# Two hybrid blocks on one core: padded rows, other banks for turned rows, an earlier overflow test, and an end by halves

## The chip, the cores and the metric

The kernel runs on one core of a Trainium2 chip (trn2). The core has five engines with a queue each: TensorE (PE: matrix products), VectorE (DVE), ScalarE (ACT), GpSimd (POOL) and SyncE (SP, which here only issues DMAs), and 16 DMA engines. They meet only through semaphores. The metric is the time of one launch in microseconds on the device, the median of the runs; lower is better.

## The reference

256 tokens of width 1024 in float32 pass through two blocks. Cut to what matters:

```python
def rms_norm(x, g):
    y = x * lax.rsqrt(jnp.mean(x * x, axis=-1, keepdims=True) + EPS)
    return y * g

def first_block(x, ...):
    h = rms_norm(x, g_mix)
    x = x + hybrid_mixer(h, w_in, ...)     # h @ w_in, two kinds of attention, gates, w_pa, w_pb, w_o
    h = rms_norm(x, g_moe)
    x = x + hier_moe(h, ...)               # top 2 of 32 experts for each token
    return rms_norm(x, g_final)

def expert_block(xblk, e):
    return (jax.nn.silu(xblk @ w1[e]) * (xblk @ w3[e])) @ w2[e]

def hybrid_layer(x, c, ...):               # the second block
    shift, scale, gate = jnp.split(silu(c) @ w_ada + b_ada, 3, axis=-1)
    h = rmsnorm(x, norm_g) * (1 + scale) + shift
    proj = h @ w_in                        # 1024 x 10240
    merged = sigmoid(m_attn) * y_attn + sigmoid(m_conv) * y_conv
    return x + gate * (merged @ w_out)

out = rmsnorm(hybrid_layer(first_block(x)), final_g)
```

## The kernel before

One program, 256 tokens as two row blocks (`n` = 0, 1) of 128. Each weight matrix comes by SP into one of five ring buffers of 2 MB (eight in the experts' part), in the order of the list `chunks`. SP issues the next load when the last user of the buffer has raised its semaphore.

*Precision by halves.* A projection's weights are cut into pieces of 128 x 1024. ACT copies a piece to a high part in fp32r (`split_high`, L1881); DVE, or GpSimd for every fourth, subtracts it from the piece to give the low part (`split_low`, L1300 on DVE, L2256 on GpSimd). TensorE multiplies high by high, high by low and low by high (`product`).

*Order.* `Order` objects `O1` (first block) and `O2` (second) are lists of steps written by hand in the Python code. Each engine's program walks the same list and takes its part of each step: TensorE multiplies, ACT and DVE evict and split. A step's place in the list sets its place in each engine's queue. `PB.use(name, bank)` gives a result one of the eight PSUM banks in turn; before TensorE writes a bank it waits until the last result in it has been read (`may_write`: semaphore `free`).

*Start.* SP loads `ident`, the two row blocks of x, `rows` (113 short vectors of 128 numbers packed as rows: gains, biases, convolution weights), then the first projection `fq` in two halves. ACT squares row block 0, DVE row block 1, GpSimd takes the inverse roots (L2244), ACT and DVE scale. TensorE first turns `rows` into columns (`col`), multiplies `ident` by itself before and after (`warm`), then turns x in four pairs (`turn1`). ACT scales each pair with the gain in `col` to the high part (L1890), DVE makes the low part (L1306). DVE copies `col` ahead of scaling row block 1.

*Experts.* Each expert has 64 slots. TensorE gathers tokens, multiplies with w1 and w3, turns, multiplies with w2 (`down`) and scatters pairs of experts into banks 2 to 5. If an expert has more tokens than slots, three more rounds of all experts follow; each engine reads the number (`flag`) and branches around that long code. ACT and DVE did this between the last expert (31) and its finish: `finish` (L2071, L2078) evicts the last down-projection on ACT, `last_low` makes its low part on DVE.

*End.* The last projection `w_out_2` comes in halves `wx0` and `wx1` of 512 columns; both need a bank per row block. DVE multiplies by the gate and adds x, GpSimd (`wx0`) or DVE (`wx1`) multiplies by the last gain, ACT squares (L2162). Then `final` takes the mean squares, GpSimd the roots, ACT scales row block 0 (L2234) and half of 1 (L2236), DVE the other half, SP stores (L890).

## Time and profile before

| | before |
|---|---|
| median of 3 runs | 1033.22 us (1032.62 to 1033.77) |
| profiled execution | 1032.23 us |
| its span | 1030.4 us |
| TensorE busy (PE) | 988.3 us, 96% |
| DVE / ACT / GpSimd busy | 392.5 / 377.1 / 121.8 us |
| mean granted TensorE clock | 0.988 of 2.4 GHz |
| DMA | 308.07 MB, mean 299 GB/s |
| chain that ended last | PE 85%, DVE 7%, ACT 4%, issue 2%, POOL 1%, DMA 1% |

The span runs from the first to the last instruction of the profile; the execution's own time has 1.8 us around it. All lines of product are in helpers: L782 is any matmul, L1300 any product or sum of two tensors on DVE, L1303 and L1306 the forms with a scalar; a row is told by its tiles and its time. "issue" is time for which the profile shows nothing that the engine waits for. `PEld` is the loading of TensorE's stationary operand. A float32 product of `ident` by itself leaves two records.

### The profile page before, as it was taken

To read this page: it belongs to the slowest core of one execution; us is meant where nothing else is said; L and a number is where in the kernel's file an instruction comes from. 1 tells how busy PE (TensorE), PEld (TensorE's weight loads), DVE (VectorE), ACT (ScalarE), POOL (GpSimd) and SP (SyncE) were. 2 spreads that over 40 slices of the span, in tenths; PEclk is the share of its full clock that TensorE was granted. 3 is DMA by queue.
4 is the path that set the end of the run, shared out by engine and by line. 5 is a ranking of instruction groups with operands and counts; after the bars stand their busy time and mean duration, and the time that the engine had idled before them with its cause. 6 is when DMAs were issued, how large, how long until landed. Compare 5 with 4: busy or idle time off the path is not lost.

```text
span 1030.4 us, 16914 instructions
## 1 busy us (share of the span) xinstructions
PE 988.3 (96%) x7393; PEld 767.3 (74%) x7393; DVE 392.5 (38%) x750; ACT 377.1 (37%) x612; POOL 121.8 (12%) x81
## 2 busy tenths in 40 slices
PE   7999999999999999979999999989999999999996
PEld 6888789976555555545555555558989999999995
DVE  4446456853222111121222111127335444774475
ACT  4545646641111111111111111226445555554443
POOL 2110021020000000000000000002321111441122
PEclk8999999999999999998999999999999999999999
DMA  8974295788999999999999999997545544445301
GB/s 271 365 273 177 96 346 217 300 315 348 424 426 425 423 425 426 426 420 426 424 425 423 427 425 424 424 401 283 184 163 187 187 171 164 164 167 204 141 1 42
DMA packets 74829, 308.07 MB, mean 299 GB/s; under 512 B 5585, under 2 KB 12146, under 8 KB 58362
## 3 DMA queue, kind: packets, MB, share of 16 engines
q1 hardware_dynamic: 70962, 302.16, 74.0%
q10 hardware_dynamic: 3784, 4.73, 1.4%
q8 instruction: 61, 1.00, 0.4%
q14 instruction: 22, 0.18, 0.1%
HBM read 305.82 MB, written 2.63 MB: 299 GB/s over the span
## 4 chain that ended last, share of the span: by engine, by line
PE 85%; DVE 7%; ACT 4%; issue 2%; POOL 1%; DMA 1%; SPq 0%; ACTq 0%; DVEq 0%
PE bank L782 82%; DVE arena L1306 3%; DVE arena L1303 2%; PE bank L1251 1%; ACT arena L2058 1%; DVE wR L1300 1%; DMA arena<-in_rows 1%; PE bank L993 1%; DVE arena L1300 1%; ACT wR L1881 1%; POOL wR L2256 1%; ACT arena L2088 0%; DVE hTR L1300 0%; ACT arena L2086 0%; ACT arena L2111 0%
## 5 line engine op out<-in xcount | busy, mean ns | idle before, releaser
L782 PE MATMUL bank<-hTR,wR 128*128 128x256 f32 x2520 | 313.8, 284 | 4.2 <-DVE wR L1300 1.2
L782 PEld LDWEIGHTS bank<-hTR,wR 128*128 128x128 f32 x2520 | 305.1, 192 | 8.2 <-issue 4.2
L782 PE MATMUL bank<-ring,arena 128*64 128x256 f32 (+3 forms) x1680 | 229.6, 439 | 7.1 <-issue 7.1
L1300 DVE TENSOR_TENSOR wR<-ring,wR 128x1024 fp32r<-128x1024 f32 x126 | 157.8, 1259 | 133.2 <-ACT wR L1881 132.6
L1881 ACT ACTIVATE wR<-ring 128x1024 fp32r<-128x1024 f32 x161 | 168.5, 1055 | 109.2 <-PE bank L782 107.4
L782 PEld LDWEIGHTS bank<-ring,arena 128*64 128x64 f32 (+2 forms) x1680 | 115.3, 137 | 103.1 <-issue 59.7
L782 PE MATMUL bank<-arena 128*64 128x256 f32 (+7 forms) x1178 | 166.5, 406 | 0.7 <-DVE small L1432 0.7
L1306 DVE SCALAR_TENSOR_TENSOR arena<-bank,small,arena 128x256 f32<-128x256 f32 x32 | 15.5, 484 | 346.9 <-ACT arena L2058 346.9
L2029 ACT ACTIVATE arena<-bank,small 64x512 f32<-64x512 f32 x62 | 42.4, 684 | 280.5 <-PE bank L782 280.1
L782 PEld LDWEIGHTS bank<-arena 128*64 128x64 f32 (+3 forms) x1178 | 92.3, 144 | 62.4 <-issue 28.3
L2256 POOL TENSOR_TENSOR wR<-ring,wR 128x1024 fp32r<-128x1024 f32 x35 | 85.5, 2443 | 321.7 <-ACT wR L1881 321.7
L2244 POOL TENSOR_TENSOR small<-small,mhalf 128x1 f32<-128x1 f32 (+1 forms) x12 | 8.2, 683 | 479.9 <-DVE small L1306 475.5
L2058 ACT ACTIVATE arena<-bank,small 128x256 f32<-128x256 f32 x32 | 15.2, 475 | 82.7 <-PE bank L782 82.7
L782 PE MATMUL bank<-wR,hTR 128*128 128x512 f32 x192 | 45.2, 393 | 0.0
L782 PEld LDWEIGHTS bank<-wR,hTR 128*128 128x128 f32 x192 | 35.6, 188 | 8.1 <-issue 0.8
L782 PE MATMUL bank<-PmR,XShR 128*128 128x256 f32 x128 | 35.9, 312 | 0.4 <-DVE small L1492 0.3
L782 PEld LDWEIGHTS bank<-PmR,XShR 128*128 128x128 f32 x128 | 24.8, 193 | 11.9 <-issue 11.2
L782 PE MATMUL bank<-PmR,XSlR 128*128 128x256 f32 x128 | 32.7, 287 | 0.0
L1303 DVE TENSOR_SCALAR arena<-bank,col 128x256 f32<-128x256 f32 x64 | 28.1, 477 | 3.4 <-PE bank L782 3.4
L1300 DVE TENSOR_TENSOR arena<-arena 128x512 f32<-128x512 f32 (+5 forms) x36 | 21.4, 604 | 10.8 <-ACT arena L2188 9.8
L1300 DVE TENSOR_TENSOR arena<-bank,arena 128x512 f32<-128x512 f32 (+2 forms) x30 | 19.6, 665 | 15.0 <-PE bank L782 12.7
L782 PEld LDWEIGHTS bank<-PmR,XSlR 128*128 128x128 f32 x128 | 25.0, 195 | 0.0
(209 smaller groups left out, 823.2 us busy)
## 6 DMA issues: line engine op xcount, KB each, us to landing
ring<-in_w SPq DMA_DIRECT2D x39, 2048.0 KB, 21.5
ring<-in_w_in SPq DMA_DIRECT2D x29, 2048.0 KB, 8.4
arena<-in_w SPq DMA_DIRECT2D x25, 2048.0 KB, 19.0
ring<-in_w SPq DMA_DIRECT2D x42, 1024.0 KB, 19.4
arena<-in_w SPq DMA_DIRECT2D x22, 1024.0 KB, 20.9
ring<-in_w_ada SPq DMA_DIRECT2D x6, 2048.0 KB, 7.9
ring<-in_w_o SPq DMA_DIRECT2D x2, 2048.0 KB, 12.4
ring<-in_w_o_attn SPq DMA_DIRECT2D x2, 2048.0 KB, 7.9
```

Of the source, the lines that this page charges most:

```text
L782: return pe.e.matmul(o, l, r, start=start, stop=stop)
L993: last = eng.transpose(banks[u.bank][:, 128 * c:128 * c + 128], P[:, 128 * c:128 * c + 128], ident[:, :])
L1251: last = eng.transpose(banks[x.bank][:, 128 * c:128 * c + 128], Hb[e % 2][:, c:256:2], ident[:, :])
L1300: return eng.tensor_tensor(o, a, b, op)
L1303: return eng.tensor_scalar(o, a, s1, s2, op0) if op1 is None else eng.tensor_scalar(o, a, s1, s2, op0, op1)
L1306: return eng.scalar_tensor_tensor(out=o, in0=a, scalar=s, in1=b, op0=op0, op1=op1)
L1881: eng.activation(h, w, ACT.Copy).then_inc(s_high, 1)
L2029: last = eng.activation(Y[h0:h0 + 64, 512 * h:512 * h + 512], banks[u.bank][64 * h:64 * h + 64, :], ACT.Copy, scale=RW[64 * h:64 * h + 64, ...
L2058: eng.activation(Hb[e % 2], banks[u.bank][:, 0:256], ACT.Silu, scale=RW[:, e // EB % 2, e % EB, 1:2]).then_inc(S["silu"], 1)
L2244: eng.tensor_tensor(o, a, mhalf[:, 0:a.shape[1]], ALU.pow).then_inc(after, 1)
L2256: eng.tensor_tensor(l, pieces[i][1], h.bitcast(F32), ALU.subtract).then_inc(low[i][0], 1)
```

## The change

- `rows` is padded on the host with zeros to 128 rows; SP loads all 128. `ident` is loaded by ACT, ahead of its first instruction, no longer by SP. The second warm-up has 3 products instead of 5.
- The turned pairs of both blocks (`hT1`, `hT3`) take banks 2 to 5, one each; before, they took 0, 1, 6 and 0 in turn. All later results that share banks 0, 1 and 6 shift by one in their turn.
- ACT and DVE test for overflow ahead of expert 31. Its code stands in both branches. TensorE's, SP's and GpSimd's tests stay.
- At the end, `wx0`'s two row blocks come one before and one behind the last weight piece's low part on DVE. For `wx1`, row block 0 is finished to its root before row block 1 is begun; ACT scales row block 0 before it squares the last half of row block 1.

```diff
         for j2 in range(4):
-            PB.use(("hT1", j2), PR.next())
+            PB.use(("hT1", j2), 2 + j2)
...
-            PB.use(("hT3", j2), PR.next())
+            PB.use(("hT3", j2), 2 + j2)
...
-        last4 = list(O2.chunk("wx1", uses, "m"))
+        last4 = O2.chunk("wx1", uses, "m")
+        first = next(last4)
+        O2.add("gate_rows", 0, 0)
+        last4 = [first] + list(last4)
+        O2.add("gate_rows", 0, 1)
         O2.add("evict", "wx0", None)
...
-        O2.add("evict", "wx1", None)
+        for n in range(NT):
+            O2.add("gate_rows", 1, n)
+            O2.add("last_squares", n)
...
         def sync_program(eng):
-            eng.dma_start(ident[:, :], t["k_ident"]).then_inc(s_ident, 16)
...
-            eng.dma_start(VR[0:NROW, :], t["rows"]).then_inc(s_rows, 16)
+            eng.dma_start(VR[:, :], t["rows"]).then_inc(s_rows, 16)
...
-            warm(pe, banks[6], 5)
+            warm(pe, banks[6], 3)
...
+                elif what == "gate_rows":
+                    c, n = a
+                    cs, u = slice(512 * c, 512 * c + 512), U_[f"wx{c}", n]
+                    filled(v, u)
+                    if c:
+                        v.wait_ge(s_gx[n], 1)
+                    tt(GT[n], banks[u.bank][:, :], grow[:, cs], ALU.mult).then_inc(u.free, 1)
+                    emptied(v, u)
+                    v.wait_ge(s_x2done[n], 1)
+                    tt(XN[:, n, cs], GT[n], XN[:, n, cs], ALU.add).then_inc(s_gx[n], 1)
+                    if c:
+                        v.wait_ge(s_gx[n], 2)
+                        v.wait_ge(s_fg, 16)
+                        v.step(tt(XO[:, n, cs], XN[:, n, cs], fg[:, cs], ALU.mult))
+                        final(n)
...
-            last_low = experts(0, PB, dict(zip(MOE_SEMS, [sem(n) for n in MOE_SEMS])))
+            S = {n: sem(n) for n in MOE_SEMS}
+            experts(0, PB, S, 0, NE - 1)
             v.wait_ge(s_flag, 1)
             with eng.If(eng.value_load(flag[0:1, 0:1]) > SLOTS):
-                last_low()
+                experts(0, PB, S, NE - 1)()
...
             with eng.Else():
-                last_low()
+                experts(0, PB, S, NE - 1)()
...
+                elif what == "last_squares":
+                    n = a[0]
+                    squares(1, n)
+                    if n == 0:
+                        s.wait_ge(s_rs[0], 4)
+                        s.wait_ge(s_fo[0], 1)
+                        eng.activation(XO[:, 0, :], XO[:, 0, :], ACT.Copy, scale=st3[:, 6:7]).then_inc(s_out[0], 2)
...
+            eng.dma_start(ident[:, :], t["k_ident"]).then_inc(s_ident, 16)
...
-            finish = experts(0, PB, dict(zip(MOE_SEMS, [sem(n) for n in MOE_SEMS])))
+            experts(0, PB, S, 0, NE - 1)
...
-    arrays["rows"] = np.concatenate([arrays.pop(n).reshape(-1, 128) for n in _ROWS])
+    rows = np.concatenate([arrays.pop(n).reshape(-1, 128) for n in _ROWS])
+    arrays["rows"] = np.concatenate([rows, np.zeros((128 - len(rows), 128), rows.dtype)])
```

The load of `ident` is taken out of SP's program and stands first in ACT's. The changed kernel's own line numbers are a few higher (L782 becomes L788, L1881 L1886).

TensorE's queue at the start, before: `ident,arena` are transposes, `hTR,wR` the first projection; `freeN` is the semaphore of PSUM bank N.

```order
L900 MATMUL bank<-ident,arena 128x113 [waits rows]
L782 MATMUL bank<-ident 128x128 x5
L987 MATMUL bank<-ident,arena 128x128 [waits norm0]
L987 MATMUL bank<-ident,arena 128x128
L987 MATMUL bank<-ident,arena 128x128 [waits norm1]
L987 MATMUL bank<-ident,arena 128x128 x9
L987 MATMUL bank<-ident,arena 128x128 [waits free0]
L987 MATMUL bank<-ident,arena 128x128 x3
L782 MATMUL bank<-hTR,wR 128x256 [waits low_dve,free1]
```

And TensorE's queue at the same place in the changed kernel:

```order
L905 MATMUL bank<-ident,arena 128x113 [waits rows]
L788 MATMUL bank<-ident 128x128 x3
L992 MATMUL bank<-ident,arena 128x128 [waits norm0]
L992 MATMUL bank<-ident,arena 128x128
L992 MATMUL bank<-ident,arena 128x128 [waits norm1]
L992 MATMUL bank<-ident,arena 128x128 x13
L788 MATMUL bank<-hTR,wR 128x256 [waits free2,low_dve]
L788 MATMUL bank<-hTR,wR 128x256 x5
L788 MATMUL bank<-hTR,wR 128x256 [waits free3]
```

No transpose waits for a bank any more, and the first product waits for the first pair (bank 2) instead of the second (bank 1).

ACT's queue round the last expert, before: L2029 evicts a down-projection, L2058 is the silu of an expert, L2038 fills the rows of gains, L2071 evicts the last down-projection.

```order
L2058 ACTIVATE arena<-bank,small 128x256 [waits full0,full6]
L2038 ACTIVATE arena<-bank 128x512 [waits full1]
L2029 ACTIVATE arena<-bank,small 64x512 [waits scat,full7]
L2029 ACTIVATE arena<-bank,small 64x512
L2058 ACTIVATE arena<-bank,small 128x256 [waits full0,full6]
L2038 ACTIVATE arena<-bank 128x512 [waits full0]
L2214 TENSOR_LOAD flag [waits flag]
L2214 COMPARE_AND_BRANCH
L2071 ACTIVATE arena<-bank,small 64x512 [waits full7]
```

And ACT's queue there now:

```order
L2064 ACTIVATE arena<-bank,small 128x256 [waits full0,full6]
L2044 ACTIVATE arena<-bank 128x512 [waits full1]
L2231 TENSOR_LOAD flag [waits flag]
L2231 COMPARE_AND_BRANCH
L2035 ACTIVATE arena<-bank,small 64x512 [waits scat,full7]
L2035 ACTIVATE arena<-bank,small 64x512
L2064 ACTIVATE arena<-bank,small 128x256 [waits full0,full6]
L2044 ACTIVATE arena<-bank 128x512 [waits full0]
L2077 ACTIVATE arena<-bank,small 64x512 [waits full7]
```

The test moved ahead of four instructions, to behind expert 30. On DVE it moved likewise ahead of the last expert's two.

DVE's queue at the end, before: `high` is the last weight piece, `full3` and `full4` are `wx0`, `full0` and `full1` `wx1`, `sq3_n` a row block's squares.

```order
L1300 TENSOR_TENSOR wR<-ring,wR 128x1024 [waits high] x5
L1300 TENSOR_TENSOR arena<-bank,arena 128x512 [waits full3]
L1300 TENSOR_TENSOR arena<-arena 128x512 [waits x2done0,free3]
L1300 TENSOR_TENSOR arena<-bank,arena 128x512 [waits full4]
L1300 TENSOR_TENSOR arena<-arena 128x512 [waits x2done1,free4]
...
L1300 TENSOR_TENSOR arena<-bank,arena 128x512 [waits gx1,full1]
L1300 TENSOR_TENSOR arena<-arena 128x512 [waits free1]
L1300 TENSOR_TENSOR arena<-arena 128x512 [waits gx1]
L1300 TENSOR_TENSOR small<-small 128x1 [waits sq3_0]
```

And DVE's queue at the end now; `wx0` is in banks 2 and 3, `wx1` in 4 and 0:

```order
L1305 TENSOR_TENSOR wR<-ring,wR 128x1024 [waits high] x4
L1305 TENSOR_TENSOR arena<-bank,arena 128x512 [waits full2]
L1305 TENSOR_TENSOR arena<-arena 128x512 [waits x2done0,free2]
L1305 TENSOR_TENSOR wR<-ring,wR 128x1024 [waits high]
L1305 TENSOR_TENSOR arena<-bank,arena 128x512 [waits full3]
...
L1305 TENSOR_TENSOR small<-small 128x1 [waits sq3_0]
L1308 TENSOR_SCALAR small<-small 128x1 [waits dve_own]
L1305 TENSOR_TENSOR arena<-bank,arena 128x512 [waits gx1,full0]
L1305 TENSOR_TENSOR arena<-arena 128x512 [waits free0]
```

The last low part now stands behind the first half of `wx0`, and row block 1 of `wx1` behind row block 0's small steps.

## Rows read from the trace of the kernel before

**Rows 1.** Stretch: us; busy PE, PEld, DVE, ACT, POOL; granted clock; DMA share, GB/s.

```profile
600.00:650.00 50.00, 48.96 (x390) 29.51 (x390) 10.63 (x28) 8.90 (x15) 0.00 (x0) 1.00 1.01 425
```

**Rows 2.** Chain of waits, 0 to 40 us: start us, us, what.

```profile
0.72 0.39 SPq L846
...
2.11 7.54 DMA arena<-in_rows
...
10.14 2.16 PE bank L782 x10
12.30 0.87 PE bank L987 x4
...
13.26 0.85 ACT hTR L1890 x2
...
16.30 0.80 DVE hTR L1306 x2
...
17.14 22.93 PE bank L782 x189
```

**Rows 3.** DMA issues of the page: size of one, us from issue to landing.

```profile
out_x<-arena SPq DMA_DIRECT2D x2, 512.0 KB, 3.0
...
ident<-in_k_ident SPq DMA_DIRECT2D x1, 64.0 KB, 2.0
```

**Rows 4.** Timeline of the start: start us, us, engine, line, operation [idle before].

```profile
4.92 1.06 ACT L2205 ACTIVATE arena<-arena 128x1024 f32<-128x1024 f32 x1 [2.92 <-DMA arena<-in_x]
...
6.40 1.23 DVE L1817 CUSTOM_DVE_ANT_0 arena<-arena 128x1024 f32<-128x1024 f32 x1 [6.40 <-DMA arena<-in_x]
...
8.41 0.56 POOL L2244 TENSOR_TENSOR small<-small,mhalf 128x1 f32<-128x1 f32 x1
...
10.37 0.74 DVE L1303 TENSOR_SCALAR arena<-arena,small 128x1024 f32<-128x1024 f32 x1
```

**Rows 5.** Loads from w_in issued in 2.4 to 3.0 us.

```profile
DMA to landing us min/median/max: 10.1/10.1/10.1
```

**Rows 6.** Busy time as in rows 1, at the start.

```profile
12.00:14.00 2.00, 2.00 (x11) 2.00 (x11) 0.00 (x0) 0.74 (x3) 0.00 (x0) 0.50 1.04 387
```

**Rows 7.** Timeline round the last expert.

```profile
680.79 1.38 ACT L2029 ACTIVATE arena<-bank,small 64x512 f32<-64x512 f32 x2 [7.65 <-PE bank L782]
...
686.94 0.48 DVE L1306 SCALAR_TENSOR_TENSOR arena<-bank,small,arena 128x256 f32<-128x256 f32 x1 [10.78 <-ACT arena L2058]
...
688.54 3.65 PE L782 MATMUL bank<-ring,arena 128*64 128x512 f32 x16 [0.56 <-issue]
...
693.47 0.68 ACT L2071 ACTIVATE arena<-bank,small 64x512 f32<-64x512 f32 x1 [5.36 <-issue]
```

**Rows 8.** Who waited for whom, 450 to 680 us: us in total, times, longest.

```profile
PE bank L782 <- issue: 6.5, 1, 6.5
```

**Rows 9.** Timeline of the end.

```profile
1014.60 1.23 DVE L1300 TENSOR_TENSOR wR<-ring,wR 128x1024 fp32r<-128x1024 f32 x1 [1.49 <-ACT wR L1881]
...
1017.78 1.28 DVE L1300 TENSOR_TENSOR arena<-arena 128x512 f32<-128x512 f32 x1
...
1019.15 1.29 POOL L2313 TENSOR_TENSOR arena<-arena 128x512 f32<-128x512 f32 x1 [0.63 <-DVE arena L1300]
...
1021.66 0.69 DVE L1300 TENSOR_TENSOR arena<-bank,arena 128x512 f32<-128x512 f32 x1
1022.39 1.42 DVE L1300 TENSOR_TENSOR arena<-arena 128x512 f32<-128x512 f32 x2
...
1024.14 1.09 POOL L2244 TENSOR_TENSOR small<-small,mhalf 128x1 f32<-128x1 f32 x2 [3.70 <-DVE small L1303]
...
1024.80 1.15 ACT L2234 ACTIVATE arena<-arena,small 128x1024 f32<-128x1024 f32 x1 [0.96 <-issue]
...
1025.85 0.71 ACT L2236 ACTIVATE arena<-arena,small 128x512 f32<-128x512 f32 x1
```

**Rows 10.** From the page: matmuls of 512 columns, busy us, mean ns.

```profile
L782 PE MATMUL bank<-wR,hTR 128*128 128x512 f32 x192 | 45.2, 393 | 0.0
```

More of the change, by code:

```diff
@@ L1577, in weights, with experts @@
                 tt(WR[:, :, :, 0], S01[0], S01[1], ALU.add).then_inc(s_weights, 1)
-            def experts(r, P, S):
+            def experts(r, P, S, lo=0, hi=NE):
                 g = max(r - 1, 0)
@@ L1609, in experts @@
                     select(0)
-                for j in range(4):
-                    gathered(0, j)
-                if not r:
-                    weights()
-                for e in range(NE):
+                if lo == 0:
+                    for j in range(4):
+                        gathered(0, j)
+                    if not r:
+                        weights()
+                for e in range(lo, hi):
                     b, k = divmod(e, EB)
@@ L1725, in second_steps @@
                            ALU.mult).then_inc(u.free, 1)
-                    elif nm in ("wx0", "wx1"):
-                        c = int(nm[2])
-                        cs = slice(512 * c, 512 * c + 512)
-                        for n in range(NT):
-                            u = U_[nm, n]
-                            filled(v, u)
-                            if c:
-                                v.wait_ge(s_gx[n], 1)
-                            tt(GT[n], banks[u.bank][:, :], grow[:, cs], ALU.mult).then_inc(u.free, 1)
-                            emptied(v, u)
-                            v.wait_ge(s_x2done[n], 1)
-                            tt(XN[:, n, cs], GT[n], XN[:, n, cs], ALU.add).then_inc(s_gx[n], 1)
-                            if c:
-                                v.wait_ge(s_gx[n], 2)
-                                v.wait_ge(s_fg, 16)
-                                v.step(tt(XO[:, n, cs], XN[:, n, cs], fg[:, cs], ALU.mult))
+                elif what == "gate_rows":
[13 more added lines that the diff above has]
+                        final(n)
                 elif what == "norm2":
@@ L1851, in vector_program @@
                     second_steps(*step)
-            final()
         def scalar_program(eng):
@@ L2018, in route, with experts @@
                 eng.activation(ex5, ex5, ACT.Exp).then_inc(s_rexp, 1)
-            def experts(r, P, S):
+            def experts(r, P, S, lo=0, hi=NE):
                 g = max(r - 1, 0)
@@ L2046, in high @@
                         eng.activation(YhR[par][:, cs], Yb[par][:, cs], ACT.Copy).then_inc(S["yhigh"], 1)
-                for e in range(NE):
+                for e in range(lo, hi):
                     if e:
@@ L2090, in second_norm, with squares @@
                 eng.activation(XV[:, 0, :], XS2[:, 0, :], ACT.Copy, scale=tw[:, 10:11]).then_inc(s_norm[0], 1)
+            def squares(c, n):
+                s.wait_ge(s_gx[n], c + 1)
+                if c:
+                    s.wait_ge(s_sq3[n], 1)
+                eng.activation(JK[n], XN[:, n, 512 * c:512 * c + 512], ACT.Square,
+                               accum_out=st3[:, 2 * n + c:2 * n + c + 1]).then_inc(s_sq3[n], 1)
             def bias(h):
@@ L2210, in scalar_program @@
             route()
-            finish = experts(0, PB, dict(zip(MOE_SEMS, [sem(n) for n in MOE_SEMS])))
+            S = {n: sem(n) for n in MOE_SEMS}
+            experts(0, PB, S, 0, NE - 1)
             s.wait_ge(s_flag, 1)
@@ L2214, in scalar_program @@
             with eng.If(eng.value_load(flag[0:1, 0:1]) > SLOTS):
-                finish()
+                experts(0, PB, S, NE - 1)()
                 s.wait_ge(s_scat, NE // 2)
@@ L2223, in scalar_program @@
             with eng.Else():
-                finish()
+                experts(0, PB, S, NE - 1)()
             s.known = known
@@ L2231, in scalar_program @@
                     second_steps(*step)
-            s.wait_ge(s_rs[0], 4)
-            s.wait_ge(s_fo[0], 1)
-            eng.activation(XO[:, 0, :], XO[:, 0, :], ACT.Copy, scale=st3[:, 6:7]).then_inc(s_out[0], 2)
             s.wait_ge(s_rs[1], 4)
```

30 lines of the change are left out of this document (12 added, 18 removed).

## The prediction

> **What bounds the kernel now.** I read the stretches of engine time first, then the chain of waits at the start, the timeline round the last expert, and the timeline of the end. In the experts' stretch TensorE is busy for 48.96 of 50 us, and the DMA engines are full too, share 1.01 at 425 GB/s [rows 1]. TensorE has no spare time there, and the change adds and removes nothing there; so from about 17 us to the end of the last expert the kernel is one long train behind TensorE, and what moves its first wagon moves all of it. What the change can win lies in three places where TensorE waits or is done: before its first projection, between the last expert's product and the last scatter, and after its last matmul.
>
> *The start.* TensorE starts its projections at 17.14 us [rows 2]. The chain back from there [rows 2] is: the load of `rows` (7.54 us, landed at 9.65), its transpose, warm-up products until 12.30, transposes of x, ACT's scaling at 13.26, DVE's low part of the first weight piece (to 16.30), DVE's second pair of `hTR`. Nothing in it is long because of arithmetic; the load is. It is 113 rows of 512 bytes, fewer than the 128 of `ident` (64 KB), which lands 2.0 us after its issue [rows 3].
>
> *The last expert.* ACT waits 5.36 us before the last down-projection is evicted, and the reason shown is "issue": nothing that the profile sees. TensorE has had that product ready since 688.54 + 3.65 = 692.19; ACT starts at 693.47 [rows 7].
>
> *The end.* TensorE's last product has ended when DVE begins at 1021.66. Then DVE (three products, to 1023.81), ACT's square, DVE's two small steps, GpSimd's two square roots (1.09 us, to 1025.23), ACT's scaling of row block 0 (1.15) and only then half of row block 1 (0.71, to 1026.56), and the last store [rows 9].
>
> **Part 1: start.** Edits that answer together: `rows` on 128 partitions, `ident` issued by ACT, three warm-up products instead of five, own banks.
> - `rows` stands behind both loads of x. x0 comes to use at 4.92 us, x1 at 6.40 [rows 4]. If `rows` spreads as `ident` does, it lands right behind x1, at about 6.5 less what x gains; as now, it lands at 9.65. I take the first: 113 rows of 512 bytes took 7.54 us, 128 rows of the same length 2.0.
> - The Trainium skill (DMA: Bandwidth & Descriptors, "Why a DMA increments its semaphore by 16 and not by 1") says that the number of DMA engines is the largest up to 16 that divides the outer sizes: one for 113 partitions, sixteen for 128. The row cannot tell one slow engine from queueing behind x; by the rule the whole excess over x goes, and so does the same engine's lateness in what follows.
> - That lateness matters: the first half of `fq`, issued at 2.49, takes 10.1 us to land (12.6 us) [rows 5]. Were it still that late, less the 0.4 that SP gains below, ACT could split it at 12.2; now it does so behind its first two scalings, at 13.26 + 0.85 = 14.1 [rows 2], so the chain would win only 1.9 us. Spread, the bytes before it are 64 + 1024 + 64 + 1024 KB, and at the 387 GB/s of rows 6 these 2.2 MB take 5.8 us. Issued from 1.1 us on, with the 2.0 of a small load ahead, it lands near 9.
> - `ident` away from SP: x is issued 0.39 + 0.06 us earlier [rows 2]. `ident` still shares the engines (64 of 576 KB), so x gains 0.25 to 0.45; I take 0.4. ACT has a spare 2 us before x arrives, so its own issue (0.4 us) is hidden; without that cover it would cost 0.4.
> - New critical path: x, squares, GpSimd's roots. The second root ends at 8.41 + 0.56 = 8.97 now, 8.57 then. DVE scales at once instead of at 10.37 (it stands behind the copy of `rows`): 8.62 + 0.74 = 9.36 [rows 4]. TensorE transposes the first four blocks by 9.85 (four take 0.87 us [rows 2], and only two of the four wait for DVE). ACT's first scaling starts at 9.9 instead of 13.26, 3.4 us earlier. DVE and ACT then do what they did: the low part of piece 0 ends at 12.9 instead of 16.30.
> - Warm-up: nine products of 0.43 us (2.16 for ten halves, rows 2) from 2.8 to 6.7, the transpose of `rows`, three more to about 8.4; TensorE then idles under 1 us before x is ready. Two fewer products win nothing themselves (they end before x is ready); they must only not delay.
> - Own banks: now the first product waits for bank 1, so for DVE's pair at 17.10, though its weights are ready at 16.30. Then it waits for the weights and pair 0 alone and starts at 12.9. But pairs 1 to 3 arrive every 0.80 us [rows 2], while six matmuls last 0.73 (22.93 / 189 each), so the first tile ends with DVE's last pair, 15.35 + 0.75 = 16.1, instead of 17.14 + 24 × 0.121 = 20.1; the second waits for its low part, 16.4, and ends at 19.4 instead of 23.0. Gain at the train: 3.6; without the banks it would be 0.2 less. For the second block's four turned pairs I take 0: there TensorE waits for DVE's split, which itself waits for ACT.
> - Value 3.5. Bounds: 1.3 if `rows` does not spread (x 0.4, two warm products, 0.5 of 0.9, half of the bank's 0.8), up to 4.1 if the root's first call also ends earlier.
>
> **Part 2: overflow tests.** The branch moves from behind the last expert's first half to before that expert. Behind it now stands the gap of 5.36 us, begun at 688.11. TensorE's own test, in the middle of the experts, leaves a gap of the same kind, 6.5 us [rows 8]. Moved, ACT's gap begins at 673.14 and ends at 678.5 to 679.7; its next input comes at 680.79 (7.65 us idle) [rows 7]. DVE's begins at about 676.2 and has until 686.94 (10.78 idle). Both covered, by 1.1 and 5 us at least. Behind the waiting branch nothing is queued that anyone needs sooner. ACT then evicts at 692.24: gain 1.23, and the chain behind it (split, scatter, norm, transposes) is ACT, DVE and TensorE in series, so nothing else is late next; the first weights of block two landed before ACT's 696. Value 1.2, bounds 0 (ready later for another reason) and 1.3. The skill (Advanced Engine Details and Errata, "Control Flow Timing") gives a compare-and-branch about 0.108 us; by that alone this edit would bring 0.1. The measured gap is fifty times that, so I go by the row.
>
> **Part 3: end by halves.** DVE has 1.49 us idle before the last low part at 1014.60 [rows 9]; one half of `wx0` (0.68 + 0.69) fits in. GpSimd's product (1.29) then starts near 1014.6 and collides with that low part: beside GpSimd, DVE's product of two SBUF tensors takes 1.28 instead of 0.69. At worst the low part waits it out and ends at 1014.6 + 1.29 + 1.23 = 1017.1; TensorE needs it some 18 matmuls of 45.2 / 192 = 0.235 us before its end, at 1017.4 [rows 9, 10]. Block 0's last half is done by 1021.1, its variance by 1021.6, just in time for block 1 at 1021.66. GpSimd's first root then runs beside DVE's block 1, and ACT scales block 0 at 1022.2 to 1023.4, which holds the last square 0.3 us. Root 1 ends at 1025.1 (now 1025.23), ACT's last half at 1025.8 instead of 1026.56: 0.75. The stores, now issued 0.6 us apart and landing 3.0 us after issue [rows 3], no longer share the engines: another 0.4 to 0.6. Value 1.2; bounds −0.3 (DVE held up behind the small steps, or the low part late) and 1.7.
>
> **Sum.** 3.5 + 1.2 + 1.2 = 5.9. The profiled execution took 1032.23 (span 1030.4 and 1.8 around it): 1026.3. The median is 1.0 above it, 1033.22: **1027.3**. With all lower bounds 1033.2 − 1.0 = 1032.2, with all upper ones 1026.1; the sixteen-engine start could bring some tenths more.
>
> **Rivals.**
> 1. *The clock is low at the start.* After TensorE's 3 us pause for `rows` its granted clock is 0.50, so 1.2 GHz, in the row from 12 to 14 us [rows 6], though it has been busy since 9.7. If the new pattern (short pause, transposes, 1.4 us pause) also leaves it low, 24 matmuls last 24 × 0.242 = 5.8 us instead of 2.9: 2.9 less. Then 1030.2. Against: the pause is under 1 us instead of 3. Chance 0.12. The skill (TensorE: Matmul & The Clock Gate, Part 1) likewise has idleness lower the clock and activity restore it.
> 2. *The start is lost in the experts' transfers*, which are full. The weights then come no earlier and TensorE catches up with them. Part 1 gives 0: 1030.8. Against: in that stretch a load is issued when TensorE frees its buffer, so the train of loads moves too, and TensorE hardly waits. Chance 0.06.
> 3. *The code behind the branch comes in two pieces.* If the last expert's code, now behind the branch, needs a second fetch, ACT pays 5.4 us between 686.9 and 692.2 on the path: 4.2 later than now, total 1032.7. If DVE's follows in series, 1038. It decides from the point where the second fetch is not begun before ACT arrives. For it: two engines show gaps of 5.4 and 6.5 us behind their branches; against: the straight code elsewhere shows none. No change 0.03, slower 0.04. The skill (Advanced Engine Details, "ISA Cache") speaks of a cache of two lines; no row here shows where one ends.
> 4. *The halves do not fit*: DVE reaches block 1 late. Part 3 gives 0: 1028.5, inside the forecast's own range.
>
> Forecast with all three parts 0.75, own range 1025.5 to 1029.3. Range at eight in ten: 1025.4 to 1030.8. A difference under 0.2% (2.1 us) can't be told from none. Faster 0.90 (forecast, most of rivals 1, 2 and 4), the same 0.05, slower 0.05.
>
> **What would show it.** `rows` transposed before 7.5 us; ACT's first `hTR` near 9.9; TensorE's first projection near 13 and the second tile's end 3.5 us earlier than now; granted clock 1.00 from 10 to 20 us. No idle "issue" before ACT's last eviction, which starts within 0.1 us of the last down-projection's end, and a gap under 7 us before it, one expert earlier. ACT's scaling of block 0 before the last square; stores more than 1.5 us apart. It is wrong if `fq` still lands 10 us after issue, if TensorE's idle in the experts grows, or if ACT shows a new idle of about 5 us in the last expert.

## The result

| | before | changed |
|---|---|---|
| median | 1033.12 us (4 runs, 1032.62 to 1033.77) | 1026.31 us (4 runs, 1025.78 to 1026.51) |
| profiled execution, span | 1032.23, 1030.4 us | 1025.78, 1024.0 us |
| mean granted TensorE clock | 0.988 | 0.991 |

The ratio of the times is 0.9932, 95% interval [0.9919, 0.9944]: 6.8 us less, where 5.9 were forecast (1027.3 us, range 1025.4 to 1030.8). The two profiled executions differ by 6.45 us, and all of it can be laid out by the time at which TensorE reaches the same product in both:

| TensorE at | before | changed | ahead by | added since |
|---|---|---|---|---|
| first projection | 17.14 | 13.81 | 3.33 | 3.33 |
| transposes ahead of the routing | 223.98 | 222.22 | 1.76 | −1.57 |
| first products of an expert | 244.40 | 241.10 | 3.30 | +1.54 |
| last down-projection | 688.54 | 684.83 | 3.71 | +0.41 |
| start of the last scatter | 695.59 | 690.64 | 4.95 | +1.24 |
| end of the span | 1030.4 | 1024.0 | 6.4 | +1.49 |

The steps of −1.57, +1.54 and +0.41 are for the most part none of the change's terms. Of the first, 1.0 us is a stretch in which the changed kernel's TensorE had a low clock (three other executions of the same start, without it, are 0.9 to 1.0 us ahead of this one at 20 to 70 us); the other 0.6 is the banks' gain at the first product, which the next tile gives back (e6). The second is a low clock in the execution of before. The third falls at TensorE's own overflow test (450 to 475 us), which the change leaves as it was, and its cost differs between executions: read at the same instructions of ACT, e7 passes it 0.36 us faster than the kernel before, whose code is the same there, and e9 1.2 us faster than the changed kernel.

**The start.** From the timeline of the changed kernel, in the columns of [rows 4]:

```profile
5.00 1.06 ACT L2221 ACTIVATE arena<-arena 128x1024 f32<-128x1024 f32 x1 [2.54 <-DMA arena<-in_x]
...
5.21 3.83 PE L788 MATMUL bank<-ident 128*128 128x128 f32 x18 [5.21 <-DMA ident<-in_k_ident]
...
8.88 0.26 PE L905 MATMUL bank<-ident,arena 113*128 113x113 f32 x1
...
9.18 0.28 DVE L1825 COPY col<-bank 128x113 f32<-128x113 f32 x1 [1.57 <-PE bank L905]
9.37 0.74 DVE L1308 TENSOR_SCALAR arena<-arena,small 128x1024 f32<-128x1024 f32 x1
...
9.66 2.26 PE L992 MATMUL bank<-ident,arena 128*128 128x128 f32 x16
...
10.71 0.84 ACT L1895 ACTIVATE hTR<-bank,col 128x256 fp32r<-128x256 f32 x2 [1.51 <-PE bank L992]
```

And its page's rows of DMA issues, as in [rows 3]:

```profile
ident<-in_k_ident ACTq DMA_DIRECT2D x1, 64.0 KB, 4.4
arena<-in_rows SPq DMA_DIRECT2D x1, 64.0 KB, 4.9
```

`rows`, issued at 1.64 us, lands 4.9 us later, at 6.5: as forecast. But its transpose stands behind nine warm-up products, and these wait for `ident`, which now takes 4.4 us instead of 2.0 and begins to be used at 5.21 instead of 2.7 us. So TensorE turns `rows` at 8.88, DVE copies the columns at 9.18, and its scaling of row block 1 (9.37), behind the copy on the same engine, starts 0.4 us after the root it needs. ACT's first `hTR` is at 10.71, not at 9.9.

**The clock.** Stretches of engine time in the changed kernel, in the columns of [rows 1]:

```profile
12.00:14.00 2.00, 0.19 (x1) 0.20 (x2) 2.00 (x4) 2.00 (x6) 0.00 (x0) 1.00 1.05 388
14.00:16.00 2.00, 2.00 (x15) 1.98 (x15) 2.00 (x6) 2.00 (x4) 0.00 (x0) 0.83 1.04 387
16.00:18.00 2.00, 2.00 (x11) 2.00 (x11) 2.00 (x3) 0.57 (x1) 0.00 (x0) 0.50 1.04 395
...
228.00:232.00 4.00, 2.97 (x26) 2.58 (x23) 3.06 (x11) 1.88 (x2) 0.00 (x0) 1.00 0.65 211
232.00:236.00 4.00, 3.90 (x33) 2.88 (x32) 3.51 (x17) 0.21 (x1) 0.00 (x0) 1.00 1.02 426
```

Rows of the same place in the kernel before, at the start of the experts:

```profile
230.00:234.00 4.00, 2.71 (x24) 2.47 (x21) 2.86 (x10) 1.88 (x2) 0.00 (x0) 1.00 0.69 231
234.00:238.00 4.00, 4.00 (x22) 3.37 (x22) 2.39 (x10) 0.21 (x1) 0.00 (x0) 0.57 1.04 434
```

In the changed kernel TensorE is almost idle from 12 to 14 us (it waits for the first low part), and then the granted clock is 0.50 (1.2 GHz) for some 3 us of projections. In the kernel before it is 0.57 in a stretch behind the routing, in which TensorE had waited for DVE; the changed kernel had the same waits 1.8 us earlier and kept its full clock. Which of these stretches an execution has is taken up below.

**The last expert.** Timeline of the changed kernel, beside [rows 7]:

```profile
677.07 1.38 ACT L2035 ACTIVATE arena<-bank,small 64x512 f32<-64x512 f32 x2 [7.65 <-PE bank L788]
...
688.52 0.68 ACT L2077 ACTIVATE arena<-bank,small 64x512 f32<-64x512 f32 x1 [4.13 <-PE bank L788]
```

TensorE's down-projection now runs from 684.83 for 3.65 us, to 688.48, and ACT starts 0.04 us later, released by TensorE and no longer by "issue". One expert earlier its 7.65 us of idle are the same as before, now with the branch inside them.

**The end.** Timeline of the changed kernel, beside [rows 9]:

```profile
1009.64 2.28 DVE L1305 TENSOR_TENSOR wR<-ring,wR 128x1024 fp32r<-128x1024 f32 x1 [0.17 <-ACT wR L1886]
...
1016.27 0.39 PE L788 MATMUL bank<-wR,mRl 128*128 128x512 f32 x1
1016.38 0.15 DVE L1308 TENSOR_SCALAR small<-small 128x1 f32<-128x1 f32 x1
1016.62 0.57 POOL L2258 TENSOR_TENSOR small<-small,mhalf 128x1 f32<-128x1 f32 x1 [1.99 <-DVE small L1308]
...
1017.27 1.15 ACT L2178 ACTIVATE arena<-arena,small 128x1024 f32<-128x1024 f32 x1 [1.11 <-issue]
...
1020.07 0.72 ACT L2250 ACTIVATE arena<-arena,small 128x512 f32<-128x512 f32 x1 [1.04 <-POOL small L2258]
```

Row block 0's root (16.62) begins as TensorE ends; its scaling is done at 18.42, and its store is issued 2.4 us before the second. From TensorE's last product (16.66) to ACT's last half (ends 20.79) it is 4.13 us instead of 4.93 before; from there to the end of the span 3.2 instead of 3.9. The stores were issued 0.6 us apart before, and now the first one's 2.7 us are nearly over when the second is issued; e5 has the 3.9 back with the old order.

### The profile page after: what moved, and what is told of

It reads as the page before. It is cut to its first block and busy times, and to the rows that moved or that the text cites. A ratio compares the mean times of both kernels' runs of the same rounds, so it can differ in the third digit from the quotient of the medians.

```text
span 1024.0 us, 16905 instructions
## 1 busy us (share of the span) xinstructions
PE 984.7 (96%) x7389; PEld 764.7 (75%) x7389; DVE 391.9 (38%) x750; ACT 376.8 (37%) x612; POOL 121.6 (12%) x81
## 5 line engine op out<-in xcount | busy, mean ns | idle before, releaser
L788 PE MATMUL bank<-hTR,wR 128*128 128x256 f32 x2520 | 315.4, 286 | 5.6 <-DVE wR L1305 3.1
L788 PEld LDWEIGHTS bank<-hTR,wR 128*128 128x128 f32 x2520 | 306.7, 192 | 9.6 <-issue 5.5
L788 PE MATMUL bank<-ring,arena 128*64 128x256 f32 (+3 forms) x1680 | 229.4, 439 | 6.8 <-issue 6.8
L1886 ACT ACTIVATE wR<-ring 128x1024 fp32r<-128x1024 f32 x161 | 168.3, 1054 | 110.5 <-PE bank L788 108.7
L788 PEld LDWEIGHTS bank<-ring,arena 128*64 128x64 f32 (+2 forms) x1680 | 115.3, 137 | 102.7 <-issue 59.3
L788 PE MATMUL bank<-arena 128*64 128x256 f32 (+7 forms) x1178 | 166.2, 406 | 0.8 <-DVE small L1437 0.7
L788 PEld LDWEIGHTS bank<-arena 128*64 128x64 f32 (+3 forms) x1178 | 92.1, 144 | 62.2 <-issue 28.1
L788 PE MATMUL bank<-wR,hTR 128*128 128x512 f32 x192 | 45.2, 393 | 0.0
L788 PEld LDWEIGHTS bank<-wR,hTR 128*128 128x128 f32 x192 | 35.6, 188 | 8.0 <-issue 0.8
L788 PE MATMUL bank<-PmR,XShR 128*128 128x256 f32 x128 | 34.9, 306 | 0.4 <-DVE arena L1308 0.4
L788 PEld LDWEIGHTS bank<-PmR,XShR 128*128 128x128 f32 x128 | 24.1, 188 | 11.7 <-issue 11.2
L788 PE MATMUL bank<-PmR,XSlR 128*128 128x256 f32 x128 | 31.7, 281 | 0.0
L788 PEld LDWEIGHTS bank<-PmR,XSlR 128*128 128x128 f32 x128 | 24.2, 189 | 0.0
## 6 DMA issues: line engine op xcount, KB each, us to landing
ring<-in_w SPq DMA_DIRECT2D x42, 1024.0 KB, 19.7
arena<-in_w SPq DMA_DIRECT2D x22, 1024.0 KB, 20.8
```

Of the source, the lines that this page charges most:

```text
L788: return pe.e.matmul(o, l, r, start=start, stop=stop)
L1886: eng.activation(h, w, ACT.Copy).then_inc(s_high, 1)
```

## The experiments

All ratios are against the kernel before, run beside each. Executions of one kernel spread over 0.7 to 5.6 us here, so medians hardly part kernels 1 us apart; each verdict is read from the profiled execution, at the same product of TensorE or the same instruction of ACT, and rests on that one execution.

**e1: `ident` by SP again.**

```diff
         def sync_program(eng):
+            eng.dma_start(ident[:, :], t["k_ident"]).then_inc(s_ident, 16)
...
-            eng.dma_start(ident[:, :], t["k_ident"]).then_inc(s_ident, 16)     (ACT)
```

> The changed kernel with one edit undone: `ident` is again the first load of SP's queue. In the changed kernel TensorE's warm-up begins at 5.21 us instead of 2.73, so `rows` is transposed at 8.88 although it may have landed earlier, DVE copies the columns at 9.18 and scales row block 1 only at 9.37, 0.44 us after the root (8.93). Theory A: the issue by ACT is the harm (its load shares the DMA engines with x and lands with it). Then here the warm-up begins near 2.8, `rows` is transposed before 8, DVE scales within 0.1 us of the root, the first projection starts 0 to 0.4 us earlier than 13.80, total 0 to 0.4 us less. Theory B (the prediction's): x comes 0.4 us later and everything with it, first projection at 14.2, total 0.4 us more.

1028.18 us (1025.68 to 1029.72), ratio 0.9943 [0.9922, 0.9964]. Timeline:

```profile
2.67 3.82 PE L788 MATMUL bank<-ident 128*128 128x128 f32 x18 [2.67 <-DMA ident<-in_k_ident]
...
6.63 0.32 PE L906 MATMUL bank<-ident,arena 113*128 113x113 f32 x1
...
9.25 0.75 DVE L1309 TENSOR_SCALAR arena<-arena,small 128x1024 f32<-128x1024 f32 x1 [1.45 <-POOL small L2258]
```

And one of its stretches:

```profile
10.00:12.00 2.00, 2.00 (x11) 1.94 (x10) 0.20 (x2) 1.15 (x3) 0.00 (x0) 0.50 1.11 355
```

Both theories hold in part and cancel. `rows` is turned at 6.63 and DVE no longer waits for the copy, but x0 comes to use at 5.07. In all profiled executions with `ident` on SP it came at 4.92 to 5.07 (three), with `ident` on ACT at 4.53 to 4.71 (ten) and once, in the changed kernel's first profile, at 5.00. So with `ident` on ACT x gains 0.4 us and `rows` loses it again: the first projection is at 13.95 here, and at 13.27 to 13.95 in the five profiled executions whose start is that of the changed kernel (its own two, e4, e5 and e8). A gain or loss by this edit can't be told inside that spread, and e1's own TensorE had a low clock while it turned x (the row above), which the others had not.

**e2: 113 rows again.** `eng.dma_start(VR[0:NROW, :], t["rows"][0:NROW, :])` in place of all 128.

> The changed kernel with one edit undone: the load of `rows` takes 113 rows again. Theory A (one DMA engine carries all 113 rows and is late with all that follows): `rows` lands 2 to 4 us later than now, the first half of `fq` at 12 us or later, first projection at 15.3 to 16.5 instead of 13.80, total 1.5 to 3 us more. Theory B (`rows` only queued behind x, and what counts is `ident` and the banks): first projection within 0.5 us of 13.80, total within 0.5 us.

1028.07 us (1026.38 to 1029.72), ratio 0.9945 [0.9926, 0.9965]. Timeline:

```profile
9.40 0.32 PE L905 MATMUL bank<-ident,arena 113*128 113x113 f32 x1 [0.84 <-DMA arena<-in_rows]
...
12.30 1.06 ACT L1886 ACTIVATE wR<-ring 128x1024 fp32r<-128x1024 f32 x1 [0.17 <-DMA ring<-in_w_in]
```

`rows` lands 2.9 us later, and ACT's first split waits for `fq`, at 12.30 (the prediction's 12.2). Yet the first projection is at 14.67, only 0.86 us later than in the changed kernel's first profile, 0.7 to 0.9 later than in e4, e5 and e8, and 1.4 later than in e11 (13.27). Neither theory's number held: the load is late, but most of what stood behind it had been shortened by the other edits.

**e7: the kernel before, `rows` padded, nothing else.**

```diff
-            eng.dma_start(VR[0:NROW, :], t["rows"]).then_inc(s_rows, 16)
+            eng.dma_start(VR[:, :], t["rows"]).then_inc(s_rows, 16)
```

> The kernel before with one edit: `rows` padded to 128 rows, all loaded. Theory A (its load is what the whole start waits for): `rows` is transposed before 8 us, the five warm-up products behind it end before x is scaled, and the first projection starts at 14.5 to 15.0 us instead of 17.14; total 2.0 to 3.0 us less. Theory B (read from the changed kernel with 113 rows, whose first projection came only 0.86 us later): 16.0 to 16.3, total about 1 us less.

1030.85 us (1029.06 to 1033.69), ratio 0.9982 [0.9966, 0.9997]. Timeline:

```profile
6.66 0.44 PE L900 MATMUL bank<-ident,arena 113*128 113x113 f32 x1
...
14.24 5.00 PE L782 MATMUL bank<-hTR,wR 128*128 128x256 f32 x27 [1.34 <-DVE hTR L1306]
```

The padding alone brings the first projection from 17.14 to 14.24: theory A, 0.3 us beyond its range. With e2, the parts of the start overlap: padding alone 2.90 us, all the others alone 2.47, together 3.33. Of the 2.0 us that both bring alone, 1.3 are TensorE's queue behind the transpose of `rows`: five warm-up products at the low clock (2.16 us, [rows 2]) stand in it before, three at the full clock (0.84) now. The other 0.7 no run tells apart.

**e6: the turned pairs in banks 0, 1, 6, 0 again.** `PB.use(("hT1", j2), PR.next())`, and so for `hT3`.

> The changed kernel with one edit undone: the turned pairs take banks 0, 1, 6 and 0 again. Theory A (the prediction's): the first projection waits for DVE's second pair, 14.5 instead of 13.8 us, but the second weight piece's tile ends at most 0.2 us later, since that tile waits for DVE's last pair in both; total 0 to 0.3 us more. Theory B: the late start stays: 0.7 us more at 20 us and in the total. A dip of the clock at the start may shift with TensorE's pause; the offsets are read with it.

1027.51 us (1026.60 to 1028.70), ratio 0.9945 [0.9927, 0.9962]. Timeline:

```profile
9.05 1.51 PE L788 MATMUL bank<-ident 128*128 128x128 f32 x6
...
11.25 0.84 ACT L1895 ACTIVATE hTR<-bank,col 128x256 fp32r<-128x256 f32 x2 [2.40 <-PE bank L992]
...
15.13 4.10 PE L788 MATMUL bank<-hTR,wR 128*128 128x256 f32 x32 [1.34 <-DVE hTR L1311]
```

From ACT's first scaling to the first projection it is 3.88 us instead of 3.10: TensorE waits for DVE's second pair, 0.78 more. Against an execution with the same start and no low clock in its first 70 us (e8's), e6's first scaling is 0.49 us later (its three warm-up products, which wait for no bank of the turned pairs, took 1.51 us instead of 0.88) and TensorE at 70 us 0.68 later: 0.19 are left for the banks. Theory A, at the value forecast; why these products were slower at a granted clock of 1.00 stays open.

**e3: the pause ahead of the first projection filled.**

```diff
                 transposes_pe(pe, eng, U_["hT1", a[0]], XS1, a[0], (s_norm[0], 1), (s_norm[1], 1))
+                if a[0] == 3:
+                    warm(pe, banks[6], 4)
```

> The changed kernel with four warm-up products of `ident` more, behind the last transpose of x, where TensorE idles from 11.92 to 13.80 us. In the changed kernel the granted clock is 0.50 from about 15.3 to 18.7 us, and of 3.3 us won at the first product 1.8 are left at the end of the second weight piece's tile. Theory A (the pause ahead of the first product brings the low clock, rival 1 of the prediction): with the pause filled the clock stays 1.00 to 20 us, the first product starts at the same 13.8 and the offset at 20 us is 3 us or more; total 1.2 to 1.6 us less. Theory B (the dip comes from elsewhere, or one of its kind comes anyway a little later): clock 0.50 for 3 us as now, total the same.

1026.36 us (1025.78 to 1029.35), ratio 0.9936 [0.9916, 0.9956]. Stretches of this kernel:

```profile
14.00:18.00 4.00, 3.84 (x30) 3.61 (x29) 4.00 (x7) 3.41 (x5) 0.00 (x0) 1.00 1.04 391
...
228.00:230.00 2.00, 1.57 (x14) 1.46 (x14) 1.81 (x5) 1.09 (x1) 0.00 (x0) 1.00 0.94 229
230.00:232.00 2.00, 2.00 (x12) 2.00 (x12) 0.55 (x2) 0.00 (x0) 0.00 (x0) 0.58 1.02 430
```

The clock stays full to 20 us, and TensorE is 1.2 us ahead of the changed kernel from there to 225 us. Then, behind the same waits as in the kernel before, the clock falls to 0.58, and from 245 us on this kernel is 0.3 us behind the changed one; TensorE's own test, cheaper here, brings it level. The first half fits theory A, the total theory B. That the four products kept the clock isn't shown by this profile alone: e4, e5, e6 and e8 keep it at 15 us without them.

**e11: the changed kernel once more.**

> The changed kernel itself once more. If the low clock at 15.3 us is part of the new start, it is here again; if it falls by chance at one of a few places (15, 74, 231 us), this execution shows another of them, as three kernels with the same start did, and the times spread over 3 us around 1026 to 1027.

1026.21 us (1025.16 to 1029.45), ratio 0.9942 [0.9924, 0.9960]. Its profile again has the low clock at the start (from 14.6 us) and no other before the middle. Three kernels with the same start (e4, e5, e8) have none there, but one at 74 us; all three turned `rows` and x at nearly the same times. e6, with the old banks, has neither. So the stretch belongs neither to this start nor to the load of `rows`: each execution gets it behind some of TensorE's pauses (at 12, 72 and 229 us), and the kernel before too (in the one that ends at 9.7 us, and behind the one of 233.4).

**e4: ACT's and DVE's tests late again.** `experts(0, PB, S)` ahead of the test and its finish behind it.

> The changed kernel with ACT's and DVE's overflow tests back between the last expert's products and its finish. Theory A: ACT again shows about 5.4 us of idle put down to "issue" before it evicts the last down-projection, which then starts 1.2 to 1.3 us after that product's end instead of 0.04; total 1.2 to 1.4 us more. Theory B: the last down-projection's eviction was late for another reason and the gap only coincided; total within 0.3 us.

1028.99 us (1028.26 to 1030.66), ratio 0.9958 [0.9943, 0.9973]. Timeline:

```profile
685.33 3.65 PE L788 MATMUL bank<-ring,arena 128*64 128x512 f32 x16 [0.56 <-issue]
...
691.20 0.68 ACT L2077 ACTIVATE arena<-bank,small 64x512 f32<-64x512 f32 x1 [6.30 <-issue]
...
693.32 0.50 PE L788 MATMUL bank<-Yh1R,PTR 128*128 128x512 f32 x1 [2.79 <-DVE Yl1R L1305]
```

Theory A in kind, and larger: the gap is 6.30 us, ACT starts 691.20 − 688.98 = 2.2 us late, TensorE waits 2.79 instead of 0.62 us, and its clock fell there as well (0.6 us more). The gap's length changes from execution to execution: 5.36 before, 6.30 here.

**e5: the end in the old order.**

```diff
+            O2.add("gate_rows", 1, n)
+        for n in range(NT):
             O2.add("last_squares", n)
```

together with both row blocks of `wx0` behind the last low part, and block 0's scaling behind the last square.

> The changed kernel with the end in the old order: both row blocks of `wx0` behind the last low part on DVE, both of `wx1` ahead of both roots, ACT's scaling of row block 0 behind the last square. Theory A (the end by halves is worth what the traces of before and after differ behind TensorE's last product, 8.80 against 7.31 us): here 8.7 to 8.9 us again, total 1.4 to 1.5 us more. Theory B (the stores, not the order, made the difference, since they no longer share the engines): 7.3 to 8.0.

1027.25 us (1026.68 to 1028.00), ratio 0.9942 [0.9921, 0.9963]. Timeline:

```profile
1016.87 0.39 PE L787 MATMUL bank<-wR,mRl 128*128 128x512 f32 x1
...
1021.49 0.70 ACT L2250 ACTIVATE arena<-arena,small 128x512 f32<-128x512 f32 x1
```

From TensorE's last product (1017.26) to the end of its span (1026.08) it is 8.82 us, and 7.31 in the changed kernel: 1.51. Theory A.

**e8: no test on TensorE.** `experts_pe(pe, eng, 0, PB, S, 0, NE)` without the branch; TensorE's part of the overflow rounds is left out.

> The changed kernel without TensorE's own overflow test in the middle of the experts and without TensorE's part of the overflow rounds. In the changed kernel the test leaves TensorE idle for 6.25 us at 455 us and a granted clock of 0.50 for 10.2 us, and the stretch from one expert's silu to the next takes 22.1 instead of 13.4 us: 8.7 us. The last experts' weights land 0.4 to 2.8 us before TensorE reads them. Theory A (the weight transfers are the bound over the experts' part as a whole, and TensorE's gap only refills the ring): the total falls by at most 1.5 us, and TensorE shows idle before the last experts that was not there. Theory B (TensorE sets the pace throughout, as its even periods suggest): the total falls by 8 to 9 us.

1025.67 us (1025.03 to 1026.20), ratio 0.9927 [0.9906, 0.9948]. Who waited for whom, TensorE, 580 to 680 us, and busy time:

```profile
PE bank L788 <- DMA ring<-in_w: 4.4, 5, 1.2
PE bank L788 <- DMA arena<-in_w: 1.9, 3, 1.4
...
640.00:680.00 40.00, 35.68 (x242) 19.94 (x240) 5.89 (x19) 7.39 (x12) 0.00 (x0) 1.00 1.01 420
```

The same stretch of the changed kernel:

```profile
640.00:680.00 40.00, 39.70 (x282) 23.03 (x278) 8.17 (x23) 8.94 (x15) 0.00 (x0) 1.00 1.01 419
```

Theory A. At 480 us TensorE is 8.1 us ahead of the changed kernel, at 684 us 0.2 behind, and between them it waits for weights; in the changed kernel the same view of waits shows none for a DMA there. Ahead of the test e8 was 0.6 us behind, so the 6.3 us gap and the 10 us of low clock behind it cost 0.4 us and not 8.7: the transfers set the length of the experts' part, and the gap only lets them get ahead.

**e9, e10, e12: three versions meant to be faster.** e9:

```diff
+            p.step(eng.tensor_tensor(mhalf[:, 7:8], mhalf[:, 6:7], mhalf[:, 0:1], ALU.pow))    (GpSimd, first)
...
-            warm(pe, banks[6], 3)
+            warm(pe, banks[6], 1)
...
+                    warm(pe, banks[6], 4)
```

and DVE's scaling ahead of its copy of `col`.

> A version meant to be faster: the changed kernel with (1) a small add and root on GpSimd at its program's start, since its first arithmetic costs 1.1 us more than the later ones (root 1.41 against 0.55 us), (2) DVE scaling row block 1 before it copies the turned `rows`, (3) one warm-up product instead of three behind the transpose of `rows`, (4) the four products of the third experiment ahead of the first projection. Theory A (the chain x, squares, roots, scaling sets the first projection): the second root ends 0.4 us earlier, transposes of x begin at about 9.1 instead of 9.66, and counted from the arrival of x0 the first projection comes 0.5 to 0.9 us earlier than in the changed kernel (13.81 - 5.00 = 8.81); total 0.5 to 1 us less, 1.5 more where its dip at the start is gone. Theory B (ACT's and DVE's queues behind set it): within 0.2 us.

1024.79 us (1024.26 to 1028.65), ratio 0.9926 [0.9907, 0.9944]; the changed kernel beside it 1026.21. The first projection is at 13.12 with x0 at 4.58, 8.54 us after x0 instead of 8.81: by the expectation's own measure little. But the start also depends on when `rows` is turned, and that moves by 0.6 us between executions of one start, above all with how long the nine warm-up products take (3.5 to 4.0 us). `rows` is turned at 8.81 here, as in e4 and e8 (8.80), whose first projections are at 13.79 and 13.86; e10, with e9's start, turns it at 8.30 and begins at 12.91, e11 at 8.34 and 13.27. Compared like that, the order brings 0.4 to 0.7 us. The clock stays full over the filled pause, and at 225 us TensorE is 1.1 us ahead of e11. A low clock at 231 us takes that, a shorter gap of TensorE's own test gives it back (1.2 us at 480), and behind the last expert 0.2 are left: the last experts now show a wait of 0.4 us for a load, again the transfers. The early root was for nothing:

```profile
1.20 0.56 POOL L2335 TENSOR_TENSOR mhalf<-mhalf 128x1 f32<-128x1 f32 x1
...
5.94 1.22 DVE L1824 CUSTOM_DVE_ANT_0 arena<-arena 128x1024 f32<-128x1024 f32 x1 [5.94 <-DMA arena<-in_x]
...
6.09 1.48 POOL L2260 TENSOR_TENSOR small<-small,mhalf 128x1 f32<-128x1 f32 x1
```

e10 adds warm-up products at 72 us (two) and in the routing (three and one).

> The version of e9 with warm-up products at two more places where TensorE waits and where a low clock followed in some executions: two ahead of `bf` 1 (about 72 us, dip at 74), three and one in the routing (about 229 and 230 us, dips at 230 to 234). Theory A (the dips follow pauses of TensorE, and filling these prevents them): no stretch of low clock before the middle of the experts, a spread between executions under 1 us instead of 3.6, and a median 1 to 2 us below the version without. Theory B (a few products are too little, or the dips do not depend on them): dips as before, the same median and spread, 0.5 us more for the products where TensorE was late.

1025.57 us (1025.21 to 1026.10), ratio 0.9928 [0.9913, 0.9942]. Its profile has no low clock at 74 us, but neither has e9's, and it has one from 229.6; the spread is 0.9 us instead of 4.4, the median 0.8 above e9's. Undecided between the theories.

e12 squares row block 1 on ACT. It keeps e9's other edits but for the early root, and has seven warm-up products instead of nine ahead of the transpose of `rows`:

```diff
+            s.wait_ge(s_x[1], 16)
+            eng.activation(XS1[:, 1, :], XN[:, 1, :], ACT.Square, accum_out=ss[:, 1:2]).then_inc(s_sq[1], 1)
```

> The version of e9 without its early root on GpSimd (there a first root took 0.56 us at 1.20 us, and the one behind x0 1.48 all the same, so it was no cost of the first call), with 7 warm-up products instead of 9 ahead of the transpose of `rows`, and with row block 1 squared by ACT, not DVE. In every trace GpSimd's first arithmetic behind x0 ends 0.05 us (a scaled sum, in e1) or 0.4 us (a root) after DVE's square of row block 1 ends, whenever it began. Theory A (the two contend: GpSimd waits while DVE's square runs): here the first root takes 0.55 us, ACT squares row block 1 from about 6.0 to 7.1, scales row block 0 from 7.1 instead of 7.6, and the second root starts within 0.5 us of the second square's end, 7.5 instead of 7.93; with x0 at 4.6 the first projection is at 12.6 to 12.9 instead of 13.12, total 0.2 to 0.5 us less than e9's 1024.8. Theory B (the long root has another cause): it takes 1.4 us again, ACT's second square only delays its scaling, first projection 13.1 to 13.5.

1026.17 us (1024.18 to 1028.27), ratio 0.9924 [0.9902, 0.9946]. Timeline:

```profile
6.16 0.56 POOL L2259 TENSOR_TENSOR small<-small,mhalf 128x1 f32<-128x1 f32 x1
...
7.93 0.30 PE L905 MATMUL bank<-ident,arena 113*128 113x113 f32 x1
...
12.48 3.33 PE L788 MATMUL bank<-hTR,wR 128*128 128x256 f32 x24 [1.00 <-DVE wR L1307]
```

Theory A for the root (0.56 us) and the start, which is the earliest of all, 0.64 us ahead of e9's. How much of the start is the shorter root and how much the two products fewer (`rows` is turned at 7.93 instead of 8.81) isn't told apart. In the total nothing of it can be told: the profiled execution had low clocks at 73 and 230 us. Neither e9, e10 nor e12 is shown to beat the changed kernel; their intervals overlap.

## Why the prediction was right

- **Start, 3.5 forecast.** Measured 3.33 at the first projection (3.87 in e11), where 4.2 were forecast (12.9 instead of 17.14), and behind the second tile, for which the 3.5 stood, 2.8: the 1.76 of this execution and the 1.0 that the clock took. The main step held: the slow load of `rows` is one of 113 partitions, and with 128 it lands at 6.5 us. `fq`'s first half lands 7.4 us after its issue, at 9.5, where near 9 was forecast. Three steps on the way were wrong. `ident` on ACT wasn't free: it landed 2.5 us later and held up the transpose of `rows` ("before 7.5 us": 8.88). The three products behind it did not "end before x is ready": x is scaled at 9.20, and the transposes of x start only behind them (9.66); in e6 slower ones moved the start by 0.5 us. And x was 0.4 us earlier, as forecast, in all other profiled executions with `ident` on ACT, but not in this one.
- **The clock.** "Granted clock 1.00 from 10 to 20 us" failed. This was rival 1, priced at 2.9 us with a chance of 0.12; it came in both profiled executions of the changed kernel and in e2 and e7, in e1 earlier (10 to 12 us), and in none of e4, e5, e6 and e8, so 0.12 was too low. It cost 1.0 us, not 2.9: the low stretch lay later than I had put it, from 15 us on, when part of the first tile was done. That the total did not suffer is luck: the execution of before lost 1.54 us to the same thing at 234 us, and 0.41 more at TensorE's own test. I had that stretch in the trace of before and had not asked whether it would come again. Without these three the two profiles differ by 6.45 + 1.0 − 1.54 − 0.41 = 5.5 us: 2.8 for the start, 1.2 for the tests and 1.5 for the end, where 3.5, 1.2 and 1.2 were forecast. The measured 6.45, and 6.8 between the medians, are more than the change itself shows, and the sum of 5.9 lies between.
- **Banks, 0.2 forecast:** 0.19 (e6).
- **Tests, 1.2 forecast:** 1.24, and 2.2 undone (e4). Rival 3 did not come: ACT and DVE show no second gap. DVE's cover was given as "5 us at least"; with the longer gap of 6.5 us that the same sentences use for ACT it is 686.94 − 682.7 = 4.2, which was enough too.
- **End, 1.2 forecast:** 1.49, and 1.51 undone (e5): 0.8 from ACT's last half (0.75 forecast) and 0.7 from the stores. The last low part did collide with GpSimd's product (2.28 us instead of 1.23) and was in time. Rival 4 did not come.
- **Rival 2** was rightly held off here, but for half a reason. What is won before the loads are in full swing stays won; what TensorE wins inside that part goes to the transfers but for the last 0.4 us (e8: at 245 us 0.6 behind the changed kernel, at 684 us 0.2).

## What to carry to other kernels

Lay out two traces at the same instruction of the bound engine, stage by stage, before crediting an edit with a total: here two clock stretches of 1.0 and 1.5 us, with opposite signs, and 0.4 us of an unchanged test lay between the terms. Where several edits shorten one wait, undo each alone and also do each alone: here they were worth 0.86 and 2.90 us for the same edit. And ask of a gap on the busiest engine what its suppliers do meanwhile: removing 8.7 us of gap and low clock brought 0.4.

## What the runs showed of the hardware

- **GpSimd waits for a DVE operation.** Its root takes 0.56 us alone, even as the first root of a launch (e9), and 1.41 to 1.52 us when DVE's square of row block 1 runs (in the changed kernel from 6.36 to 7.61, the root from 6.61 to 8.02); with the square on ACT it takes 0.56. In e1 a step of 0.19 us, begun 0.03 us behind the square, took 1.25, to 0.05 us after the square's end. The Trainium skill (SBUF — State Buffer, "SBUF: two separate sides") says that the port pair shared by the two is an exclusive lock, held for the whole instruction, and that a DVE operation with two SBUF inputs takes it against a GpSimd operation that reads SBUF. By that, the one that starts first makes the other wait. These rows agree, and so does the end of the changed kernel, the other way round: GpSimd's product began 0.1 us ahead of DVE's last low part, which took 2.28 us instead of 1.23. One row doesn't: in e7 a GpSimd step of 0.19 us began 0.02 us ahead of the square, which took no longer for it (1.24 us).
- **The clock falls in stretches that come and go between executions of one start.** After like pauses it fell at 15 us in two executions of the changed start and stayed full in three, which then lost it at 74 us. The Trainium skill (TensorE: Matmul & The Clock Gate, Part 1) lets idleness throttle the clock and activity release it; the rows agree in that each low stretch follows a pause, but not every pause was followed by one. With four products in the pause before the first projection all four kernels kept the clock there (e3, e9, e10, e12), without them four of nine profiled executions lost it: that the products keep it is likely, not shown.
- **A branch's gap has no fixed length:** 5.36 and 6.30 us for the same branch of ACT (before and e4), 5.9 to 6.5 for TensorE's, with the DMA engines full (share 1.01).
- **A small load issued beside large ones lands with them:** the 64 KB of `ident` took 2.0 us ahead of x on SP's queue, 4.0 to 4.4 us issued by ACT at the time of x (e2 and the changed kernel).
